# Pairwise heads in the hybrid layers of a two-block transformer kernel on one Trainium2 core

## The chip, the cores and the metric

The kernel runs on one core of one Trainium2 chip. Its time is the device time of one execution in microseconds; a comparison uses the median of several runs. Engines are named as in the profile: PE (TensorE), DVE (VectorE), ACT (ScalarE), POOL (GpSimd), SP (the queue that issues the DMAs).

## What is computed

Batch 1, 512 tokens, width 1024, everything in float32. The first block (two layers with feed-forward parts, one stick-breaking attention, one recurrent mixer) isn't touched. The second block is two hybrid layers and a norm. One hybrid layer, cut to what matters:

```
h = rmsnorm_2(x, norm_g)
proj = h @ w_in                      # a_q a_k a_v a_g  b_q b_k b_v b_g  i_q i_k i_w  c_q c_k c_v c_g  m_g
ya = moba_attention(rope(a_q), rope(a_k), a_v)            # 6 heads of 64, causal at this length
yb = dsa_attention(rope(b_q), rope(b_k), b_v, rope(i_q), rope(i_k), i_w)   # 6 heads, one key head; top 128 keys by an index score
yc = dilated_mixture(rope(c_q), rope(c_k), c_v)           # 3 groups x 4 heads, dilation 1, 4, 16; groups mixed by their log sums
merged = sigmoid(m_g)[0] * ((ya * silu(a_g)) @ w_br_a) + ... b ... + ... c ...
x = x + merged @ w_out
```

Each head is a softmax attention: scores, row maximum, exponentials with row sums, division by the sum, product with the values.

## The kernel before, in words

Every engine has its own hand-written program (`tensor`, `scalar`, `vector`, `gpsimd`, `sync`), and these meet by named semaphore steps. The order of the work is thus the order in which each program's loops are written; an engine that waits holds back all that is behind it.

Weight products are split: a panel of 256 weight columns (1 MB) is loaded by SP, rounded by ACT (`w_high`, L1239), the remainder taken by DVE (`w_low`, L1772), and PE makes three matmuls for each of the eight k-tiles and each half of the panel (48 matmuls 128x512, L594, in `product`). There are three `w_high` buffers and four raw ones.

In `hybrid(layer)` (stages `h0` and `h1`) the heads come after six panels. There are 24 heads in `L.heads`: six A, six B, then four C for each of three groups. A step `i` of the loop runs, on PE: `turns(i - 2)` (transposes of the finished weights, L1064), the panel of `L.fills` if there is one (16 of them stand beside the heads: queries, keys, values and gates of the heads to come), `scores(i + 1)` (L1048 for A and B, L1041 and L1044 for C), `values(i - 2)` (L1086, L1082). A and B heads are causal triangles of 1280 columns (TRI); C heads have 896 or 512.

On DVE a step runs `row_max(i)` (scores from PSUM with scale and mask, L2287; maxima, L2292 and L2295), `weights(i - 1)` (L2300, L2303), the rope arithmetic of the last panel (L2195 to L2199), `w_low` of the next one, up to six `some` rounds (L2237, L2239: the top keys for B, 48 rounds in all, 27 of them beside heads), and the gate of a finished pair of heads (L2342, L1958). On ACT: `turned_copy(i - 2)` (L1591: transposed weights back into the one buffer `L.PT`), `exps(i - 1)` (L1597), eviction of the panel (L1534 for rope, L1540 for gates), `w_high` of the next one. DVE copies 256 of the 1280 transposed columns (L2313). The scores of a head lie in PSUM columns 0 to 1279, its transposed weights in 1280 to 2559; bank 5 takes the products with the values, banks 6 and 7 the panels. Head dimension is 64, so a score matmul uses one half of the array's rows and a value matmul one half of its columns, in the code by `r0`:

```
m = e.matmul(flat[:, ROW_AT[n]:ROW_AT[n] + P * (n + 1)], L.q_of(kind, ti)[r0:r0 + HD, n * P:(n + 1) * P], ...)
m = e.matmul(psum[r0:r0 + HD, OUT, kt * P:S], L.v_of(kind, h, kt), L.PT[:, COL_AT[kt]:COL_AT[kt] + S - P * kt], ...)
```

The first block's attention (`stick_breaking`, stage `sb`) already takes its heads two by two; its value matmuls (L870) alternate between the two heads of a pair.

After the heads every engine meets at a fence, and PE turns the log sums (L1145).

## Time and profile before

| | |
|---|---|
| median of 3 runs | 3378.89 us (3375.52 to 3392.6) |
| the profiled execution | 3381.35 us, its span 3379.6 us |
| PE busy | 3220.0 us, 95% of the span |
| DVE busy | 1769.8 us, 52% |
| ACT busy | 1168.1 us, 35% |
| mean granted TensorE clock | 0.969 |

A busy matmul engine isn't one at its peak: matmuls overlap in the records, so that their start-to-start distance is their price. The chain that ended last is 84% PE, 9% DVE and 4% ACT.

### The profile page before, as it was taken

To read this page: it belongs to the slowest core of one execution; us is meant where nothing else is said; L and a number is where in the kernel's file an instruction comes from. 1 tells how busy PE (TensorE), PEld (TensorE's weight loads), DVE (VectorE), ACT (ScalarE), POOL (GpSimd) and SP (SyncE) were. 2 spreads that over 40 slices of the span, in tenths; PEclk is the share of its full clock that TensorE was granted. 3 is DMA by queue.
4 is the path that set the end of the run, shared out by engine and by line. 5 is a ranking of instruction groups with operands and counts; after the bars stand their busy time and mean duration, and the time that the engine had idled before them with its cause. 6 is when DMAs were issued, how large, how long until landed. Compare 5 with 4: busy or idle time off the path is not lost.

```text
span 3379.6 us, 38726 instructions
## 1 busy us (share of the span) xinstructions
PE 3220.0 (95%) x16353; PEld 2662.9 (79%) x16353; DVE 1769.8 (52%) x2488; ACT 1168.1 (35%) x1532; POOL 167.5 (5%) x228
## 2 busy tenths in 40 slices
PE   6999999999999999999999998889989998899899
PEld 5888888798888888887888887656768886567688
DVE  6545543355555543367632346875553458755534
ACT  4222356532223223247421233333442332335322
POOL 0000012200000000012000000000000010000000
PEclk8999999999999999999999998989989999899899
DMA  6555421135554432232222322221212232222132
GB/s 220 185 189 191 133 88 51 38 113 176 194 178 150 162 125 93 88 110 71 92 91 96 100 75 82 80 74 53 67 58 92 81 95 76 69 63 70 56 100 69
DMA packets 287270, 354.23 MB, mean 105 GB/s; under 512 B 9546, under 2 KB 263290, under 8 KB 287098
## 3 DMA queue, kind: packets, MB, share of 16 engines
q1 hardware_dynamic: 287098, 351.75, 32.1%
q8 instruction: 130, 2.13, 0.3%
q14 instruction: 42, 0.34, 0.0%
HBM read 336.52 MB, written 2.10 MB: 100 GB/s over the span
## 4 chain that ended last, share of the span: by engine, by line
PE 84%; DVE 9%; ACT 4%; issue 1%; DMA 1%; POOL 1%; SPq 0%; DVEq 0%; ACTq 0%; POOLq 0%
PE psum L594 56%; PE psum L753 6%; PE psum L711 3%; PE psum L1181 3%; PE psum L635 2%; PE psum L615 2%; PE psum L1048 2%; PE psum L1086 2%; PE psum L851 1%; DVE w_low L1772 1%; PE psum L1064 1%; DVE area L2239 1%; DVE psum L1921 1%; PE psum L560 1%; DVE h_low L1931 1%
## 5 line engine op out<-in xcount | busy, mean ns | idle before, releaser
L594 PE MATMUL psum<-h_high,w_high 128*128 128x512 f32 x2400 | 947.8, 395 | 27.9 <-DVE y_plain L2206 11.6
L594 PE MATMUL psum<-h_low,w_high 128*128 128x512 f32 x2400 | 941.0, 392 | 0.0
L594 PE MATMUL psum<-h_high,w_low 128*128 128x512 f32 x2400 | 940.2, 392 | 0.0
L1772 DVE TENSOR_TENSOR w_low<-raw,w_high 128x2048 fp32r<-128x2048 f32 (+2 forms) x246 | 547.6, 2235 | 301.0 <-ACT w_high L1239 300.8
L1239 ACT CAST w_high<-raw 128x2048 fp32r<-128x2048 f32 (+3 forms) x254 | 464.5, 1841 | 521.5 <-DMA raw<-in_ffn_w_gu 234.6
L594 PEld LDWEIGHTS psum<-h_high,w_high 128*128 128x128 f32 x2400 | 454.1, 189 | 131.9 <-DVE y_plain L2206 12.1
L594 PEld LDWEIGHTS psum<-h_high,w_low 128*128 128x128 f32 x2400 | 453.9, 189 | 97.3
L594 PEld LDWEIGHTS psum<-h_low,w_high 128*128 128x128 f32 x2400 | 454.1, 189 | 94.9 <-issue 1.0
L594 PE MATMUL psum<-y_high,w_high 128*128 128x512 f32 x592 | 232.9, 393 | 7.5 <-DVE y_low L1958 3.6
L2044 DVE TENSOR_TENSOR area<-area,psum 128x512 f32<-128x512 f32 x88 | 60.2, 684 | 340.1 <-PE psum L594 331.7
L594 PE MATMUL psum<-y_high,w_low 128*128 128x512 f32 x592 | 231.4, 391 | 0.0
L594 PE MATMUL psum<-y_low,w_high 128*128 128x512 f32 x592 | 231.3, 391 | 0.0
L1308 ACT CAST y_high<-area 128x512 fp32r<-128x512 f32 x102 | 62.7, 620 | 442.3 <-DVE area L2044 403.1
L1963 DVE SCALAR_TENSOR_TENSOR xT<-psum,gain_out,xT 128x512 f32<-128x512 f32 (+1 forms) x156 | 90.7, 623 | 199.4 <-PE psum L594 159.3
L1789 DVE SCALAR_TENSOR_TENSOR mod_acc<-raw,vec,mod_acc 128x1024 f32<-128x1024 f32 x112 | 143.9, 1285 | 60.8 <-DMA raw<-in_mod_w 55.6
L711 PE MATMUL psum<-h_high,w_high 128*128 128x256 f32 x448 | 133.1, 297 | 10.4 <-DVE h_low L1931 4.6
L753 PE MATMUL psum<-y_high,w_high 128*128 128x256 f32 x480 | 138.2, 288 | 0.1
L594 PEld LDWEIGHTS psum<-y_high,w_high 128*128 128x128 f32 x592 | 111.7, 189 | 32.2 <-ACT y_high L1308 4.0
L753 PE MATMUL psum<-y_high,w_low 128*128 128x256 f32 x480 | 136.4, 284 | 0.0
L753 PE MATMUL psum<-y_low,w_high 128*128 128x256 f32 x480 | 136.4, 284 | 0.0
L594 PEld LDWEIGHTS psum<-y_high,w_low 128*128 128x128 f32 x592 | 111.7, 189 | 23.7
L594 PEld LDWEIGHTS psum<-y_low,w_high 128*128 128x128 f32 x592 | 111.7, 189 | 23.1 <-issue 0.2
(301 smaller groups left out, 4584.4 us busy)
## 6 DMA issues: line engine op xcount, KB each, us to landing
raw<-in_ffn_w_gu SPq DMA_DIRECT2D x88, 1024.0 KB, 5.6
raw<-in_mod_w SPq DMA_DIRECT2D x64, 1024.0 KB, 5.0
raw<-in_w_in SPq DMA_DIRECT2D x64, 1024.0 KB, 5.2
raw<-in_ffn_w_down SPq DMA_DIRECT2D x32, 1024.0 KB, 7.4
raw<-in_ffn_w_down SPq DMA_DIRECT2D x16, 768.0 KB, 4.7
raw<-in_sb_w_qkv SPq DMA_DIRECT2D x12, 1024.0 KB, 5.1
area<-area SPq DMA_DIRECT2D x92, 128.0 KB, 2.3
raw<-in_lru_w_in SPq DMA_DIRECT2D x10, 1024.0 KB, 5.3
```

The lines of the kernel that those rows point to most:

```text
L594: mm = e.matmul(psum[0:width, base + m, :], wv[a][:, at_k, c0:c0 + width], X[b][:, k, :], start=(at_k == 0 and (a, b) == (0, 0)), stop=(at ...
L615: mm = e.matmul(psum[:, base + m, :], wv[a][:, at_k, m * P:(m + 1) * P], X[b][:, k, :], start=(at_k == 0 and (a, b) == COMBOS[0]), stop=(a ...
L635: mm = e.matmul(flat[:, o:o + n], X[b][:, k, tt * P:(tt + 1) * P], wv[a][:, k, :], start=(k == 0 and (a, b) == (0, 0)), stop=(k == KD - 1 ...
L711: mm = e.matmul(psum[:, base + m, HALF[h]], wv[a][:, k, m * P:(m + 1) * P], H[b][:, k, HALF[h]], start=first, stop=last)
L753: mm = e.matmul(psum[:, bank, m * S // 2:(m + 1) * S // 2], wv[a][:, at_k, m * P:(m + 1) * P], X[b][:, k, HALF[h]], start=(at_k == 0 and ( ...
L1048: m = e.matmul(flat[:, ROW_AT[n]:ROW_AT[n] + P * (n + 1)], L.q_of(kind, ti)[r0:r0 + HD, n * P:(n + 1) * P], L.k_of(kind, h)[:, 0:P * (n + ...
L1086: m = e.matmul(psum[r0:r0 + HD, OUT, kt * P:S], L.v_of(kind, h, kt), L.PT[:, COL_AT[kt]:COL_AT[kt] + S - P * kt], start=kt == 0, stop=kt = ...
L1181: mm = e.matmul(psum[:, base + m, :], wv[x][:, k, m * P:(m + 1) * P], Y[y][:, k, :], start=(k == k0 and (x, y) == (0, 0)), stop=(k == k1 - ...
L1239: e.copy(w_high[x % NW][:, :n], raw[raw_at[m]][:, :n]).then_inc(*q.up(s_high, "w_high", x))
L1772: e.tensor_tensor(w_low[raw_at[m]][:, :n], raw[raw_at[m]][:, :n], w_high[x % NW][:, :n].bitcast(F32), ALU.subtract).then_inc(*q.up(s_low, ...
L1789: g = e.scalar_tensor_tensor(mod_acc[:, :], w, c, mod_acc[:, :], ALU.mult, ALU.add)
L1963: return e.scalar_tensor_tensor(dst, src, gain_out[:, j:j + 1], dst, ALU.mult, ALU.add)
```

## The change

`L.heads` becomes `L.pairs`, twelve pairs of heads in another order of kinds: A A A, C C (dilation 1), B B B, C C (4), C C (16). A step handles two heads: both their scores, all their transposes, both products with the values. Matmuls of head 0 (array rows or columns 0 to 63) and head 1 (64 to 127) alternate. The scores of a pair take five banks, and the transposed weights go back into those same banks for A, B and C of dilation 1 (`turned_at`), so that `turn_weights(p)` waits until DVE has taken the scores of pair `p + 1`, and `scores(p + 2)` until ACT has copied the transposed weights of `p`. ACT copies all columns, back into the softmax buffers (four now, `L.PT` is gone). A panel's two halves (`panel_tiles`) stand at two places of a step, by the table `L.beside`; `w_high` and `w_low` are made two panels ahead, not one. The panels are loaded in another order. `dilated_mask`, ropes and gates move with them. Before and after the heads nothing changes.

```diff
-        IN_HEADS = ((("b_q", 0), 256), (("b_q", 256), 256), (("b_g", 0), 256), (("b_g", 256), 128), (("c_q", 0), 256), (("c_k", 0), 256),
-                    (("c_v", 0), 256), (("c_q", 256), 256), (("c_k", 256), 256), (("c_v", 256), 256), (("c_q", 512), 256),
+        IN_HEADS = ((("c_q", 0), 256), (("c_k", 0), 256), (("b_g", 256), 128), (("b_q", 0), 256), (("b_q", 256), 256), (("c_v", 0), 256),
+                    (("b_g", 0), 256), (("c_q", 256), 256), (("c_k", 256), 256), (("c_v", 256), 256), (("c_q", 512), 256),
                     (("c_k", 512), 256), (("c_v", 512), 256), (("m_g", 0), 256), (("m_g", D), 256), (("c_g", 0), 256), (("m_g", 2 * D), 256))
...
-            L.SS, L.PT, L.score = [tiles(ss + TRI * i, TRI) for i in range(3)], tiles(pt, TRI), tiles(sc, TRI)
+            L.SS, L.score = [tiles(ss + TRI * i, TRI) for i in range(4)], tiles(sc, TRI)
...
-            L.heads = [(kind, h, 0) for kind in "AB" for h in range(6)] + [("C", h, g) for g in range(3) for h in range(4)]
-            L.fills = {0: ("rope", "b_q", 0), 1: ("rope", "b_q", 256), 2: ("gate", "b_g", 0), 4: ("gate", "b_g", 256), 5: ("rope", "c_q", 0),
-                       6: ("rope", "c_k", 0), 8: ("tokens", "c_v", 0), 9: ("rope", "c_q", 256), 12: ("rope", "c_k", 256),
-                       13: ("turned", "c_v", 256), 15: ("rope", "c_q", 512), 16: ("rope", "c_k", 512), 18: ("turned", "c_v", 512),
-                       20: ("merge", "m_g", 0), 21: ("merge", "m_g", D), 23: ("gate", "c_g", 0)}
...
+            L.pairs = ([("A", ti, 0) for ti in range(3)] + [("C", ti, 0) for ti in range(2)] + [("B", ti, 0) for ti in range(3)]
+                       + [("C", ti, g) for g in (1, 2) for ti in range(2)])
+            L.beside = {
+                -1: ([("c_q", 0, (0, 1))], []),
+                0: ([("c_k", 0, (0, 1))], [("b_g", 256, (0,))]),
+                1: ([("b_q", 0, (0, 1))], [("b_q", 256, (0,))]),
+                2: ([("b_q", 256, (1,))], [("b_q", 256, "turn"), ("c_v", 0, (0,))]),
+                3: ([("c_v", 0, (1,))], [("b_g", 0, (0,))]),
+                4: ([("b_g", 0, (1,))], [("c_q", 256, (0,))]),
+                5: ([("c_q", 256, (1,))], [("c_k", 256, (0,))]),
+                6: ([("c_k", 256, (1,))], [("c_v", 256, (0, 1))]),
+                7: ([("c_v", 256, "turn")], [("c_q", 512, (0, 1))]),
+                8: ([("c_k", 512, (0, 1))], [("c_v", 512, (0,))]),
+                9: ([("c_v", 512, (1,))], [("c_v", 512, "turn")]),
+                10: ([("m_g", 0, (0, 1))], [("m_g", D, (0,))]),
+                11: ([("m_g", D, (1,))], [("c_g", 0, (0, 1))]),
+                12: ([], []),
+            }
...
+            def score_at(p, x):
+                kind, ti, g = L.pairs[p]
+                return x * (TRI if kind != "C" else 1024 if g == 0 else 512)
+            def turned_at(p, x):
+                kind, ti, g = L.pairs[p]
+                return score_at(p, x) + (1024 if kind == "C" and g else 0)
...
+                def scores(p):
+                    kind, ti, g = L.pairs[p]
+                    if p:
+                        for x in range(2):
+                            q.wait_ge(*at("scores_taken", stage, p - 1, x))
+                    if p > 1:
+                        for x in range(2):
+                            q.wait_ge(*at("turned_taken", stage, p - 2, x))
...
+                        for x, n in ((0, 1), (1, 3), (0, 3), (1, 2), (0, 2), (1, 0), (0, 0), (1, 1)):
+                            if (x, n) == (1, 1):
+                                q.wait_ge(*at("scores_begun", stage, p))
+                            r0, o = x * HD, L.score_at(p, x) + ROW_OF[x][n]
+                            m = e.matmul(flat[:, o:o + P * (n + 1)], L.q_of(kind, ti)[r0:r0 + HD, n * P:(n + 1) * P],
+                                         L.k_of(kind, 2 * ti + x)[:, 0:P * (n + 1)], start=True, stop=True)
+                            if (x, n) == (0, 1):
+                                m.then_inc(*q.up(s_attend, "scores_begun", stage, p))
+                    m.then_inc(*q.up(s_attend, "scores", stage, p))
...
+                def turn_weights(p):
+                    for x in range(2):
+                        q.wait_ge(*at("weights", stage, p, x))
+                    if p:
+                        for x in range(2):
+                            q.wait_ge(*at("turned_taken", stage, p - 1, x))
+                    if p + 1 < n_pairs and L.turned_at(p, 0) == 0:
+                        for x in range(2):
+                            q.wait_ge(*at("scores_taken", stage, p + 1, x))
+                    shared = L.pairs[p][0] != "C"
+                    for x in range(2):
+                        blocks = L.turns(p, x)
+                        for i, (src, dst) in enumerate(blocks):
+                            o = L.turned_at(p, x) + dst
+                            m = e.transpose(flat[:, o:o + P], L.SS[2 * (p % 2) + x][:, src:src + P], ident[:, :])
+                            if (x, i) == ((1, 1) if shared else (0, len(blocks) - 1)):
+                                m.then_inc(*q.up(s_turn, "weights_turned", stage, p, 0))
+                    m.then_inc(*q.up(s_turn, "weights_turned", stage, p, 1))
...
+                            for x in range(2):
+                                c = COL_OF[x][kt]
+                                m = e.matmul(psum[x * HD:(x + 1) * HD, OUT, kt * P:S], L.v_of(kind, 2 * ti + x, kt), w[x][:, c:c + S - P * kt],
+                                             start=kt == 0, stop=kt == NT - 1, skip_group_check=True)
+                    m.then_inc(*q.up(s_attend, "head_out", stage, p))
...
-                scores(0)
-                for i in range(n_heads + 2):
-                    if i >= 2:
-                        turns(i - 2)
-                    fill_rest(i - 1)
-                    fill(i)
-                    if i + 1 < n_heads:
-                        scores(i + 1)
-                    if i >= 2:
-                        values(i - 2)
...
+                for p in range(-1, n_pairs):
+                    if p + 1 < n_pairs:
+                        scores(p + 1)
+                    beside(p, 0)
+                    if p >= 0:
+                        turn_weights(p)
+                    beside(p, 1)
+                    if p >= 0:
+                        values(p)
...
+                def cast(p, w):
+                    for name, c0 in L.begun(p, w):
+                        split_to(two_ahead_of(number[stage, name, c0]))
+                def turned_copy(p, x):
+                    top = L.width(p)
+                    q.wait_ge(*at("weights_turned", stage, p, x))
+                    o = L.turned_at(p, x)
+                    e.copy(L.SS[2 * (p % 2) + x][:, 0:top], flat[:, o:o + top]).then_inc(*q.up(s_act, "turned_taken", stage, p, x))
...
-                n_heads = len(L.heads)
-                for i in range(n_heads + 2):
-                    if i >= 2:
-                        turned_copy(i - 2)
-                    if 1 <= i <= n_heads:
-                        exps(i - 1)
-                    fill_rest(i - 1)
-                    fill(i)
-                    if i >= 2:
-                        finish(i - 2)
...
+                for p in range(-1, n_pairs + 1):
+                    beside(p - 1, 1)
+                    cast(p, 0)
+                    if p >= 1:
+                        finish(p - 1)
+                    if p + 1 < n_pairs:
+                        for x in range(2):
+                            exps(p + 1, x)
+                        for x in range(2):
+                            log_sum(p + 1, x)
+                    beside(p, 0)
+                    if 0 <= p < n_pairs:
+                        for x in range(2):
+                            turned_copy(p, x)
+                    cast(p, 1)
...
+                rounds_of, n_pairs = {-1: 3, 0: 7, 1: 4, 2: 6}, len(L.pairs)
...
+                def take_scores(p, x):
+                    kind, ti, g = L.pairs[p]
+                    buf, width, o = L.SS[2 * (p % 2) + x], L.width(p), L.score_at(p, x)
...
+                    if p > 1:
+                        q.wait_ge(*at("head_out", stage, p - 2))
+                    runs = [(0, ROW_AT[1], o + 2 * P), (ROW_AT[1], TRI, o)] if kind != "C" and x else [(0, width, o)]
+                    for a, b, at_ in runs:
+                        m = e.scalar_tensor_tensor(buf[:, a:b], flat[:, at_:at_ + b - a], SCALE, mask[:, a:b], ALU.mult, ALU.add)
+                    m.then_inc(*q.up(s_vec, "scores_taken", stage, p, x))
...
-                n_heads = len(L.heads)
-                for i in range(n_heads + 2):
-                    if i >= 2:
-                        turned_copy(i - 2)
-                    if i < n_heads:
-                        row_max(i)
-                    if 1 <= i <= n_heads:
-                        weights(i - 1)
-                    fill_rest(i - 1)
-                    fill(i)
-                    if i in beside:
-                        beside[i]()
-                    if i >= 2:
-                        finish(i - 2)
...
+                for p in range(-1, n_pairs + 1):
+                    if p + 1 < n_pairs:
+                        for x in range(2):
+                            take_scores(p + 1, x)
+                    if p >= 1:
+                        gate_out(p - 1)
+                    if p + 1 < n_pairs:
+                        for x in range(2):
+                            row_max(p + 1, x)
+                    beside(L.early(p))
+                    lows(p, 0)
+                    if p + 1 < n_pairs:
+                        for x in range(2):
+                            weights(p + 1, x)
+                    beside(L.rest(p))
+                    if p >= 1:
+                        finish(p - 1)
+                    if p + 1 < n_pairs:
+                        for x in range(2):
+                            lse_add(p + 1, x)
+                    lows(p, 1)
+                    some(rounds_of.get(p, 0))
+                    if p == 3:
+                        select()
```

What moves on PE, in the first hybrid layer. Before, at the second and third A head (scores L1048, values L1086 of one head, transposes L1064 of the next):

```order
L1048 MATMUL psum<-area 128x128
L1048 MATMUL psum<-area 128x256
L1048 MATMUL psum<-area 128x384
L1048 MATMUL psum<-area 128x512
L1086 MATMUL psum<-area 64x512
L1086 MATMUL psum<-area 64x384
L1086 MATMUL psum<-area 64x256
L1086 MATMUL psum<-area 64x128
L1064 MATMUL psum<-ident,area 128x128 x10
```

Now, at the first A pair's values (L1173) and the third pair's scores (L1119), between two panels:

```order
L1173 MATMUL psum<-area 64x512 x2
L1173 MATMUL psum<-area 64x384 x2
L1173 MATMUL psum<-area 64x256 x2
L1173 MATMUL psum<-area 64x128 x2
L1119 MATMUL psum<-area 128x256
L1119 MATMUL psum<-area 128x512 x2
L1119 MATMUL psum<-area 128x384 x2
L1119 MATMUL psum<-area 128x128 x2
L1119 MATMUL psum<-area 128x256
```

Each value matmul now stands next to its twin of the other head, and the eight score matmuls of two heads are interleaved with sizes that differ.

On ACT, before, at two B heads (rope eviction L1534, transposed copy L1591, exponentials L1597):

```order
L1534 COPY area<-psum 128x1024
L1591 COPY area<-psum 128x1024
L1597 ACTIVATE area,mod_acc<-area,mod_acc 128x128
L1597 ACTIVATE area,mod_acc<-area,mod_acc 128x256
L1597 ACTIVATE area,mod_acc<-area,mod_acc 128x384
L1597 ACTIVATE area,mod_acc<-area,mod_acc 128x512
L1308 CAST y_high<-y_plain 128x512
```

Now, at the step of a B pair (L1719 exponentials, L1651 rope eviction, L1712 transposed copies, L1356 `w_high`):

```order
L1719 ACTIVATE area,mod_acc<-area,mod_acc 128x128
L1719 ACTIVATE area,mod_acc<-area,mod_acc 128x256
L1719 ACTIVATE area,mod_acc<-area,mod_acc 128x384
L1719 ACTIVATE area,mod_acc<-area,mod_acc 128x512
L1651 COPY area<-psum 128x1024
L1712 COPY area<-psum 128x1280 x2
L1356 CAST w_high<-raw 128x2048
```

The transposed copies of a pair stood ahead of the next exponentials and now stand behind both heads' exponentials and the eviction.

On DVE, now, the same step (L2418 scores taken, L2428 and L2431 maxima, L2436 and L2439 weights, L1901 `w_low`):

```order
L2418 SCALAR_TENSOR_TENSOR area<-psum,area 128x1280
L2418 SCALAR_TENSOR_TENSOR area<-psum,area 128x1024
L2418 SCALAR_TENSOR_TENSOR area<-psum,area 128x256
L2428 TENSOR_REDUCE mod_acc<-area 128x1 x4
L2431 TENSOR_SCALAR mod_acc<-mod_acc 128x4
L2428 TENSOR_REDUCE mod_acc<-area 128x1 x4
L2431 TENSOR_SCALAR mod_acc<-mod_acc 128x4
L2436 RECIPROCAL mod_acc<-mod_acc 128x4
```

The 12 copies of 256 columns per layer (L2313) are gone from DVE, and each second A or B head's scores are taken in two instructions.

## Rows read from the trace of the kernel before

**Rows 1.** The page: span, and busy time of the engines.

```profile
span 3379.6 us, 38726 instructions
...
PE 3220.0 (95%) x16353; PEld 2662.9 (79%) x16353; DVE 1769.8 (52%) x2488; ACT 1168.1 (35%) x1532; POOL 167.5 (5%) x228
```

**Rows 2.** Timeline of PE, where the heads begin and end, both layers.

```profile
2155.67 0.55 PE L1048 MATMUL psum<-area 64*128 64x128 f32 x1 [4.76 <-DVE y_plain L2206]
...
2491.13 2.72 PE L1145 MATMUL psum<-ident,mod_acc 128*4 128x128 f32 x12 [1.10 <-ACT area L1659]
...
2822.65 0.76 PE L1048 MATMUL psum<-area 64*128 64x128 f32 x2 [5.94 <-DVE y_plain L2206]
...
3152.70 0.58 PE L1145 MATMUL psum<-ident,mod_acc 128*4 128x128 f32 x2 [1.10 <-ACT area L1659]
```

**Rows 3.** Busy times in the first layer's heads (us, PE, PEld, DVE, ACT, POOL, PEclk, DMA).

```profile
2151.00:2490.00 339.00, 303.24 (x1424) 227.18 (x1424) 209.45 (x422) 137.33 (x290) 17.65 (x23) 0.93 0.22 64
```

**Rows 4.** Timeline of PE: the end of a panel and one B head.

```profile
2273.01 0.39 PE L594 MATMUL psum<-h_low,w_high 128*128 128x512 f32 x1
2273.24 0.39 PE L594 MATMUL psum<-h_high,w_low 128*128 128x512 f32 x1
2273.56 2.42 PE L1048 MATMUL psum<-y_plain 64*128 64x128 f32 x8
2275.91 2.37 PE L1086 MATMUL psum<-area 128*64 128x512 f32 x8
2278.21 1.31 PE L1064 MATMUL psum<-ident,area 128*128 128x128 f32 x10
```

**Rows 5.** Timeline of PE: the scores of one C head of dilation 1.

```profile
2371.68 1.83 PE L1041 MATMUL psum<-area 64*128 64x128 f32 x14
```

**Rows 6.** Timeline of PE: values of a pair in the first block.

```profile
524.26 0.64 PE L870 MATMUL psum<-area 128*64 128x512 f32 x1
524.27 0.64 PE L870 MATMUL psum<-causal,area 128*64 128x512 f32 x1
...
526.57 0.50 PE L851 MATMUL psum<-sb_parts,neg_parts 128*128 128x512 f32 x1
```

**Rows 7.** Timeline of DVE: first two A heads, the work beside them.

```profile
2160.42 1.49 DVE L2287 SCALAR_TENSOR_TENSOR area<-psum,causal 128x1280 f32<-128x1280 f32 x1 [5.01 <-PE psum L1048]
...
2163.72 2.29 DVE L1772 TENSOR_TENSOR w_low<-raw,w_high 128x2048 fp32r<-128x2048 f32 x1
2165.92 0.42 DVE L2237 MAX8 small<-area 128x8 f32<-128x256 f32 x1
...
2169.29 0.42 DVE L2237 MAX8 small<-area 128x8 f32<-128x256 f32 x1
...
2180.39 0.17 DVE L2300 RECIPROCAL mod_acc<-mod_acc 128x4 f32<-128x4 f32 x1
...
2181.79 0.68 DVE L2196 TENSOR_TENSOR area<-area,rope_s 128x512 f32<-128x512 f32 x1
...
2185.05 2.28 DVE L1772 TENSOR_TENSOR w_low<-raw,w_high 128x2048 fp32r<-128x2048 f32 x1
```

**Rows 8.** Timeline of DVE: a dilated rope, from its first instruction to the next `w_low`.

```profile
2403.62 0.68 DVE L2196 TENSOR_TENSOR area<-area,rope_s 128x512 f32<-128x512 f32 x1
...
2408.12 2.28 DVE L1772 TENSOR_TENSOR w_low<-raw,w_high 128x2048 fp32r<-128x2048 f32 x1
```

**Rows 9.** Timeline of ACT: gate eviction, transposed copy, exponentials of an A head.

```profile
2230.63 1.28 ACT L1540 ACT_TABLE_LOAD   x1
...
2238.51 1.01 ACT L1591 COPY area<-psum 128x1024 f32<-128x1024 f32 x1 [4.68 <-PE psum L1064]
2239.41 0.40 ACT L1597 ACTIVATE area<-area,mod_acc 128x128 f32<-128x128 f32 x1
...
2241.61 1.89 ACT L1239 CAST w_high<-raw 128x2048 fp32r<-128x2048 f32 x1
```

**Rows 10.** Timeline of PE: an A head's scores after a wait.

```profile
2228.24 4.63 PE L1048 MATMUL psum<-area 64*128 64x128 f32 x8 [3.44 <-DVE area L2287]
```

More of the change, by code:

```diff
@@ new lines, in hybrid_views, with last_tile, begun, done @@
+            kinds = {"b_g": "gate", "c_g": "gate", "m_g": "merge", "c_v": "turned"}
+            L.what = lambda name, c0: "tokens" if (name, c0) == ("c_v", 0) else kinds.get(name, "rope")
+            def last_tile(name, c0):
+                return 0 if (name, c0) == ("b_g", 256) else 1
+            def begun(p, w):
+                return [(name, c0) for name, c0, ms in L.beside[p][w] if ms != "turn" and 0 in ms]
+            def done(p, w):
+                if p < -1:
+                    return []
+                return [(name, c0) for name, c0, ms in L.beside[p][w] if ms != "turn" and last_tile(name, c0) in ms]
@@ new lines, in turned, with early, rest @@
+            def turned(p, w):
+                if p < -1:
+                    return []
+                return [(name, c0) for name, c0, ms in L.beside[p][w] if ms == "turn"]
+            put_off = [("c_q", 0), ("c_k", 0)]
+            def early(p):
+                out = [u for u in (done(p - 1, 0) if p > -1 else []) if u in put_off]
+                return out + (done(p - 1, 1) if p > -1 else [])
+            def rest(p):
+                return [u for u in done(p, 0) if u not in put_off]
+            L.begun, L.done, L.turned, L.early, L.rest, L.last_tile = begun, done, turned, early, rest, last_tile
@@ new lines, in beside, with gate_out @@
+                def beside(units):
+                    for name, c0 in units:
+                        what = L.what(name, c0)
+                        if what == "rope":
+                            place = L.place_of.get((name, c0))
+                            rope_rest(name, c0, *([] if place is None else [("scores_taken", stage, place, x) for x in range(2)]))
+                        if what == "gate":
+                            gate_rest(name, c0)
+                def gate_out(p):
+                    kind, ti, g = L.pairs[p]
+                    if kind == "C":
+                        return
```

444 lines of the change are left out of this document (221 added, 223 removed).

## The prediction

> **What bounds the kernel now.** I read the page first. PE is busy for 95% of the span [rows 1] and holds 84% of the chain that ended last, so a gain must shorten PE's program or its waits. The change touches only the heads of the two hybrid layers. On PE's timeline these run from 2155.67 to 2491.13 us and from 2822.65 to 3152.70: 335.5 and 330.1 us [rows 2], a fifth of the span. Both ends are matmuls of lines that stay, so I count from the one to the other.
>
> Then I priced PE's work in there, by distances from start to start. A panel's matmul takes 0.23 us, a full panel of 48 of them 11.1 [rows 4]. One A or B head takes 2.35 for scores, 2.30 for values and 1.07 for ten transposes (1.31 less the tail of the last) [rows 4]. A C head of dilation 1 takes 1.76 for its 14 score records, 0.126 each [rows 5]; I take that price for the other C matmuls: about 1.75 for values, 1.0 and 1.0 in a dilated head, with 0.107 per transpose. With 15.5 panels that is 172 + 12 x 5.7 + 4 x 4.3 + 8 x 2.45 + 2.5 for turned value columns = 280 us. The stretch takes 335, so 55 us are waits and low clock. DVE is busy for 209 of 339 us and ACT for 137, and the granted clock is 0.93 on average [rows 3]. Nothing else is full, but DVE's 209 are bunched: the key-selection rounds lie beside the first heads.
>
> **The change, part by part.** *Matmuls side by side.* A pair's two heads use different halves of the array. The first block shows what that is worth: two value matmuls start at 524.26 and 524.27, and a pair's whole set is done at 526.57, 2.3 us after it began [rows 6], which is what one head takes in the hybrid layer [rows 4]. So values halve. Scores have mixed sizes in an order where each head's pieces sum to 1280 columns; I take them as halved too. Bounds: 2.35 per A or B pair if they overlap fully, 4.7 if not. The saving per layer is 6 x (2.35 + 2.30) + 2 x 3.5 + 4 x 2.0 = 43 us; if scores do not overlap at all it is 21. PE's floor falls to 280 - 43 = 237 us per layer.
>
> *Can DVE follow?* Prices from its timeline: taking an A head's scores and its maxima 3.3 (of it 1.5 for the taking), `w_low` 2.2, three rounds 3.37, so 1.12 each, weights 1.4, a rope panel 3.3 [rows 7], or 4.5 when dilated [rows 8]. The gating of a pair costs about 1.2, from the same widths. A pair with C of dilation 1 costs 4.6 and 2.5 in place of 6.6 and 2.8, by its 896 of 1280 columns. By the new tables, DVE's steps cost
> -1: 6.6 + 2.8 + 1.5 `w_low` 3.3 + 3 rounds 3.4 = 16;
> 0: 6.6 + 2.8 + rope 3.3 + 4.4 + 7 rounds 7.8 = 25;
> 1: 6.6 + 2.8 + two ropes and a gate 7.1 + 4.4 + 4 rounds 4.5 + 1.2 = 27;
> 2: 4.6 + 2.5 + 3.3 + 2.2 + 6 rounds 6.7 + 1.5, and 1.4 of waiting for exponentials = 22;
> 3: 4.6 + 2.5 + 2.2 + 7 rounds and the mask 9.1 + 1.5 + 1.4 = 21.
> That is 111 us, where PE has 95 us of work in the same steps. So DVE becomes the bound there. `w_low` also stands behind a cast that ACT makes after its transposed copies; in steps 0 and 3 DVE gets there first, 5 us together. Removing the 256-column copies saves DVE some 5 us per layer, half of it in this stretch (already left out above).
>
> *The new waits.* `turn_weights(p)` waits for the taking of pair p + 1 and `scores(p + 2)` for the copies of p, which stand behind both exponentials on ACT. So a step can't be shorter than: taking 3.0, first maxima 1.8, two heads' exponentials at 2.2 [rows 9], an eviction 1.0, two copies of 1280 columns at 1.15 (0.9 per 1024 [rows 9]), values 2.3, scores 2.35, hops 0.6: 17.8 us. Steps 0 to 3 are longer anyway. Steps 4 and 5 have only 14 to 17.5 us of DVE work, so the loop bounds them: 18.6 (the gate eviction with table loads, 1.28 each [rows 9], makes it longer, C's narrower copies shorter) and 17.8. A panel's half stands between transposes and values, and hides nothing beyond 5.5 us.
>
> *The rest.* From there on DVE has 10 to 20 us per step beside 18 to 23 of PE, and PE is the bound: 105 us of matmuls, with about 5 of waits, chiefly for the rope of `c_k` 512, whose queries and keys are due one step after their panel (eviction 1.0, swap DMA, rope 4.5, against 7.5 us of PE work). At the end the last gate is evicted on ACT between two table loads before the last output copy, and the fence waits for it: 5 us, where now it waits 1.1 [rows 2]. POOL's and SP's moved steps (ropes' cosine, swaps, loads) have far more room: POOL is busy for 18 of 339 us [rows 3].
>
> *The clock.* After a wait of 3.4 us an A head's scores took 4.63 us, twice the 2.42 of a full clock [rows 10, 4]: the lower level, 1.2 GHz. New waits of 3 to 6 us stand in steps 2 to 5. Where DVE is the bound this costs nothing, in the loop of steps 4 and 5 it does; I add 6 us (bounds 0 and 25, the latter if turning, values and scores run at half clock in every loop and some panels behind them).
>
> **The sum.** Per layer 5 (first scores, slow as now [rows 10]) + 111 + 5 + 36.4 + 110 + 5 + 6 = 278 us. That is 57 less than 335.5 and 52 less than 330.1, together 109. From the profiled execution's 3381.35 us this gives 3272; its own time lies 2.5 above the median of the runs, so I forecast **3270 us**, 3.2% faster. About 0.5% is what a measurement of this kernel can tell from no change.
>
> **The rivals.**
> *PE bound throughout.* If DVE's backlog were absorbed by the depth of the pipeline, the layer would take 237 + 10 = 247 us, and the kernel 3381 - 171 = 3210. Against it: the banks are shared, so PE can be at most one pair ahead. Chance 0.07.
>
> *Copies bound it.* The transposed copies are ACT's alone now, and every A, B and early C step closes a loop through them. If hops, evictions and low clock make that loop 24 us rather than 17.8, steps 2 to 7 gain nothing from DVE's spare time: 20 us more per layer, 3310. For it: these waits did not exist; ACT idles long before L1591 today [rows 9]. Against it: only two steps have less DVE work than 17.8. The Trainium skill, TensorEngine Tiling (Array Packing), section PSUM Bottleneck, says that tiling speeds up TensorE but not the evacuation of PSUM, which may then become the bound, and advises sharing it between ScalarE and VectorE; the change does the opposite, and by this rule the time would be this rival's. Chance 0.2.
>
> *The pairs do not overlap.* If alternating matmuls ran one after another, the 43 us would stay on PE; DVE's bound hides some 20 of them. 278 + 23 to 278 + 43 gives 3315 to 3355. The first block speaks against it for values [rows 6]; for scores nothing shown is as clear. Chance 0.08.
>
> *Slower: the clock stays low.* More waits per matmul could keep PE at 1.2 GHz. The stage breaks even when 55 us are lost; as about 25 us of slack take up the first losses, some 80 of its 237 us of matmuls have to run at half clock that now run at full. If all 140 us up to step 6 did, the layer would take 278 + 115 and the kernel 3500. Against it: today's section waits as much (55 of 335 us) and is still granted 0.93 [rows 3]. The Trainium skill's page TensorE: Matmul & The Clock Gate, section HAM oscillation, warns of just this, bursts of matmuls between waits, each begun at the lower clock; the trace has single cases of it [rows 10], no lasting one. Chance 0.05.
>
> **How the numbers follow.** Forecast 0.6, PE bound 0.07, copies 0.2, no overlap 0.08, slow clock 0.05. The range takes the forecast's bounds (loop and clock at +25 per layer: 3320; scores cheap and DVE quick at -22 per layer: 3226), which holds the copies' case too: 3225 to 3325. Left out are most of the first, third and fourth rival. Faster by over 0.5% is everything but the slow clock and a strip around no change: 0.93; same 0.02, slower 0.05.
>
> **What would show it.** In the new profile: each layer's heads shortened to about 278 us; pair values at 2.3 us and pair scores near 2.4; DVE without gaps until some 120 us into the heads, PE waiting there for it at the transposes; then PE dense from the third B pair on; a wait near 5 us before the log sums. Pair scores near 4.7, or a granted clock under 0.85 in the heads, would speak for the rivals. Equal lengths of the two layers' gains show that nothing outside matters; a change before 2155 us or behind the fence would prove me wrong about the scope.

## The result, and the profile after

The changed kernel takes **3336.9 us** (3335.7 to 3342.5), the kernel before 3381.9 beside it: ratio 0.987, 95% interval 0.984 to 0.990. It is faster, by 45 us (1.3%) and not by the 109 forecast, and lies above the range.

Of the page of the changed kernel these rows answer to [rows 1]; the group of panel matmuls and the chain are added:

```profile
span 3334.6 us, 38716 instructions
...
PE 3123.2 (94%) x16353; PEld 2617.1 (78%) x16353; DVE 1752.0 (53%) x2476; ACT 1173.2 (35%) x1532; POOL 180.1 (5%) x228
...
PE 77%; DVE 13%; ACT 5%; DMA 1%; issue 1%; POOL 1%; SPq 1%; DVEq 0%; ACTq 0%; POOLq 0%
...
L1204 PE MATMUL psum<-h_high,w_high 128*128 128x512 f32 x464 | 194.1, 418 | 78.8 <-DVE y_plain L2335 45.0
```

PE is busy for 97 us less than before (3220.0), but the span falls by 45.0 only: half of the saved work came back as waits. The last row says where PE waits, for 78.8 us in all: before matmuls of L1204, the heads' panels, and most of it for DVE's gating at L2335. My sum has no such term.

PE's timeline from the first scores to the transposes of the log sums, as in [rows 2]. For the first layer these are all waits over 2 us ahead of its instructions, but for one of 3.13 us at 2273.03 for DVE's taking of scores; of the second layer only the first and the last row are shown:

```profile
2155.24 1.22 PE L1119 MATMUL psum<-area 64*128 64x256 f32 x3 [5.05 <-DVE y_plain L2335]
...
2211.62 0.76 PE L1204 MATMUL psum<-h_high,w_high 128*128 128x512 f32 x1 [14.09 <-DVE y_plain L2335]
...
2250.91 0.69 PE L1221 MATMUL psum<-ident,area 64*128 64x64 f32 x4 [4.39 <-ACT area L1651]
...
2279.88 0.77 PE L1204 MATMUL psum<-h_high,w_high 128*128 128x512 f32 x1 [4.52 <-ACT area L1740]
...
2307.61 0.77 PE L1204 MATMUL psum<-h_high,w_high 128*128 128x512 f32 x1 [8.14 <-DVE y_plain L2335]
...
2329.53 0.47 PE L1204 MATMUL psum<-h_high,w_high 128*128 128x512 f32 x1 [2.46 <-ACT area L1651]
...
2353.83 0.76 PE L1204 MATMUL psum<-h_high,w_high 128*128 128x512 f32 x1 [5.39 <-ACT area L1651]
...
2378.19 0.47 PE L1204 MATMUL psum<-h_high,w_high 128*128 128x512 f32 x1 [3.37 <-ACT area L1764]
...
2414.91 1.44 PE L1111 MATMUL psum<-area,y_plain 64*128 64x128 f32 x10 [3.06 <-DVE area L2328]
...
2469.54 1.47 PE L1262 MATMUL psum<-ident,mod_acc 128*4 128x128 f32 x12 [2.41 <-ACT area L1783]
...
2798.58 1.23 PE L1119 MATMUL psum<-area 64*128 64x256 f32 x3 [5.92 <-DVE y_plain L2335]
...
3109.22 1.04 PE L1262 MATMUL psum<-ident,mod_acc 128*4 128x128 f32 x8 [2.42 <-ACT area L1783]
```

The heads take 314.3 and 310.6 us: 21.2 and 19.4 less than in [rows 2], where 278 was forecast. That is 40.6 of the 45.0 us; of the rest 2.5 lie between the two layers' heads and 1.5 behind them. Inside the first layer's heads PE is busy for 258.6 us instead of 303.3 and idle for 55.7 instead of 32.2. Seven waits between 2211 and 2379, 42.4 us together, stand before a panel's first matmul (or, at L1221, before the small transposes that use the same banks). All panels and these transposes go through one pair of PSUM banks, 6 and 7, and `wait_free(6)` holds PE until the panel before has been taken out of them. Both banks come free together, by the one eviction or gating that stands behind the panel's second half.

DVE's timeline shows why the longest of them lasts 14 us. The panel of `b_g` 256 was full long before; its gating is the instruction of L2335:

```profile
2200.54 2.94 DVE L2418 SCALAR_TENSOR_TENSOR area<-psum,causal 128x1280 f32<-128x1280 f32 x3
2203.40 0.68 DVE L2471 TENSOR_TENSOR y_plain<-y_plain,psum 128x512 f32<-128x512 f32 x1
2203.99 1.66 DVE L2428 TENSOR_REDUCE mod_acc<-area 128x1 f32<-128x128 f32 x4
...
2207.53 0.69 DVE L2325 TENSOR_TENSOR area<-area,rope_s 128x512 f32<-128x512 f32 x1
...
2210.79 0.68 DVE L2335 TENSOR_TENSOR y_plain<-y_plain,psum 128x512 f32<-128x512 f32 x1
...
2230.13 0.69 DVE L2325 TENSOR_TENSOR area<-area,rope_s 128x512 f32<-128x512 f32 x1 [13.67 <-DMA area<-area]
...
2241.92 2.08 DVE L2418 SCALAR_TENSOR_TENSOR area<-psum,mod_acc 128x896 f32<-128x896 f32 x2
```

The 0.68 us of gating stand in `early(1)`, behind seven rounds of step 0, then the taking of the third pair's scores, a pair's gating, maxima and a rope. PE starts `b_q` 0 only at 2211.62. Then DVE itself waits 13.67 us, for the swap of that late panel (the DMA that a rope needs ahead of its arithmetic), and the engine that I thought full in step 1 is idle for a third of it.

On ACT's timeline the wait of 5.39 us looks so (L1719 are exponentials, L1651 the eviction of `c_q` 256; PE ran that panel's second half from 2339.83 to 2345.57):

```profile
2331.53 1.92 ACT L1356 CAST w_high<-raw 128x2048 fp32r<-128x2048 f32 x1
2346.55 0.62 ACT L1425 CAST y_high<-y_plain 128x512 fp32r<-128x512 f32 x1 [13.10 <-DVE y_plain L2471]
2348.33 0.40 ACT L1719 ACTIVATE area<-area,mod_acc 128x128 f32<-128x128 f32 x1 [1.16 <-DVE mod_acc L2431]
...
2352.70 0.99 ACT L1651 COPY area<-psum 128x1024 f32<-128x1024 f32 x1
```

ACT is idle for 13 us, nearly all of it while the panel is still being computed, so it is not overloaded. Yet the eviction comes 7 us after the panel is complete, since it stands in program order behind a cast and both heads' exponentials, which wait 1.16 us for DVE first.

The matmuls themselves are as forecast (PE's timeline: scores, values, scores of C with dilation 1, transposes, each of a whole pair):

```profile
2171.63 2.43 PE L1119 MATMUL psum<-area 64*128 64x256 f32 x16
...
2232.39 2.37 PE L1173 MATMUL psum<-area 128*64 128x512 f32 x16
2234.70 1.83 PE L1111 MATMUL psum<-area 64*128 64x128 f32 x28
...
2244.14 2.38 PE L1140 MATMUL psum<-ident,area 128*128 128x128 f32 x20 [1.93 <-DVE area L2418]
```

A pair's scores take 2.43 us, where one head took 2.42; values 2.37 for 2.37; C's 28 records 1.83, where 14 took 1.83 [rows 4, 5]. (The trace has two records for each of these matmuls on half of the array, and one for each transpose.) The window over the heads, in the columns of [rows 3]:

```profile
2151.00:2470.00 319.00, 259.09 (x1429) 206.83 (x1430) 202.34 (x415) 142.31 (x291) 17.75 (x17) 0.91 0.24 69
```

### The profile page after: what moved, and what is told of

The parts are those of the page before. It is cut to its first block, busy times and chain, and to the rows that moved or that the text cites. A ratio compares the mean times of both kernels' runs of the same rounds, so it can differ in the third digit from the quotient of the medians.

```text
span 3334.6 us, 38716 instructions
## 1 busy us (share of the span) xinstructions
PE 3123.2 (94%) x16353; PEld 2617.1 (78%) x16353; DVE 1752.0 (53%) x2476; ACT 1173.2 (35%) x1532; POOL 180.1 (5%) x228
## 4 chain that ended last, share of the span: by engine, by line
PE 77%; DVE 13%; ACT 5%; DMA 1%; issue 1%; POOL 1%; SPq 1%; DVEq 0%; ACTq 0%; POOLq 0%
PE psum L654 48%; PE psum L1204 7%; PE psum L813 6%; PE psum L771 3%; PE psum L1298 3%; PE psum L675 2%; DVE w_low L1901 2%; DVE area L2368 2%; ACT area L1719 1%; PE psum L695 1%; PE psum L911 1%; DVE small L2366 1%; DVE area L2418 1%; DVE psum L2050 1%; DVE mod_acc L2428 1%
## 5 line engine op out<-in xcount | busy, mean ns | idle before, releaser
L654 PE MATMUL psum<-h_high,w_high 128*128 128x512 f32 (+1 forms) x1936 | 759.5, 392 | 9.5 <-DVE w_low L1901 4.0
L654 PE MATMUL psum<-h_high,w_low 128*128 128x512 f32 (+1 forms) x1936 | 755.9, 390 | 0.0
L654 PE MATMUL psum<-h_low,w_high 128*128 128x512 f32 (+1 forms) x1936 | 755.7, 390 | 0.0
L1901 DVE TENSOR_TENSOR w_low<-raw,w_high 128x2048 fp32r<-128x2048 f32 (+2 forms) x246 | 547.8, 2236 | 357.1 <-ACT w_high L1356 357.0
L1356 ACT CAST w_high<-raw 128x2048 fp32r<-128x2048 f32 (+4 forms) x254 | 464.7, 1843 | 525.2 <-DMA raw<-in_ffn_w_gu 237.4
L654 PEld LDWEIGHTS psum<-h_high,w_high 128*128 128x128 f32 (+1 forms) x1936 | 364.2, 188 | 90.2 <-issue 6.2
L654 PEld LDWEIGHTS psum<-h_high,w_low 128*128 128x128 f32 (+1 forms) x1936 | 363.9, 188 | 77.4
L654 PEld LDWEIGHTS psum<-h_low,w_high 128*128 128x128 f32 (+1 forms) x1936 | 364.4, 188 | 76.8 <-issue 1.0
L1204 PE MATMUL psum<-h_high,w_high 128*128 128x512 f32 x464 | 194.1, 418 | 78.8 <-DVE y_plain L2335 45.0
L1204 PE MATMUL psum<-h_low,w_high 128*128 128x512 f32 x464 | 188.8, 407 | 0.0
L1204 PE MATMUL psum<-h_high,w_low 128*128 128x512 f32 x464 | 188.2, 406 | 0.0
L1204 PEld LDWEIGHTS psum<-h_high,w_high 128*128 128x128 f32 x464 | 92.5, 199 | 104.4 <-issue 83.9
```

The lines of the kernel that those rows point to most:

```text
L654: mm = e.matmul(psum[0:width, base + m, :], wv[a][:, at_k, c0:c0 + width], X[b][:, k, :], start=(at_k == 0 and (a, b) == (0, 0)), stop=(at ...
L1204: mm = e.matmul(psum[:, 6 + m, :], wv[a][:, k, m * P:(m + 1) * P], H[b][:, k, :], start=(k == 0 and (a, b) == COMBOS[0]), stop=(k == KD - ...
L1356: e.copy(w_high[x % NW][:, :n], raw[raw_at[m]][:, :n]).then_inc(*q.up(s_high, "w_high", x))
L1901: e.tensor_tensor(w_low[raw_at[m]][:, :n], raw[raw_at[m]][:, :n], w_high[x % NW][:, :n].bitcast(F32), ALU.subtract).then_inc(*q.up(s_low, ...
```

## The experiments

Two theories stood after the result. **Banks**: the time is lost where banks 6 and 7 wait for an eviction or a gating that stands behind the next pair's softmax on an in-order engine; moving that instruction gives it back. **DVE load**: DVE's work in steps -1 to 3 sets the pace and the bank waits are where it shows; moving work about on DVE brings nothing. A third, from the forecast's rivals, was that ACT's copies bound the later steps. The kernel before took 3378.9 to 3381.9 us beside them.

| run | on top of | us | ratio, 95% interval | first layer's heads, us |
|---|---|---|---|---|
| changed kernel | | 3336.9 | 0.987 (0.984 to 0.990) | 314.3 |
| e1_gate_early | changed | 3319.9 | 0.981 (0.979 to 0.983) | 304.0 |
| e2_evict_first | changed | 3312.9 | 0.979 (0.977 to 0.981) | 297.8 |
| e5_both | e1 and e2 | 3292.8 | 0.973 (0.971 to 0.975) | 288.0 |
| e7_both_gate0 | e5 | 3275.5 | 0.969 (0.967 to 0.971) | 280.6 |
| e10_best | e7 | 3262.7 | 0.965 (0.963 to 0.967) | 273.9 |
| e3_serial | changed | 3371.3 | 0.997 (0.995 to 0.999) | 329.0 |
| e11_serial | e7 | 3309.0 | 0.978 (0.976 to 0.981) | 298.0 |
| e4_no_rounds | changed | 3305.0 | 0.977 (0.975 to 0.979) | 295.1 |
| e6_both_no_rounds | e5 | 3248.8 | 0.961 (0.959 to 0.964) | 266.4 |
| e8_dve_copies | changed | 3338.3 | 0.987 (0.985 to 0.990) | 315.0 |
| e9_one_ahead | e7 | 3279.9 | 0.970 (0.968 to 0.972) | 283.1 |

### e1: the gate of `b_g` 256 one place earlier

```diff
-                    beside(L.early(p))
+                    beside([u for u in L.early(p) if u != ("b_g", 256)])
...
                     some(rounds_of.get(p, 0))
+                    if p == 0:
+                        beside([("b_g", 256)])
```

> The changed kernel, except that DVE does the gate of panel b_g 256 at the end of step 0 instead of behind the next pair's scores, maxima and rope. Theory 'banks' (PE's next panel can't start until ACT and DVE have emptied banks 6 and 7, and they come to it late): the 14.1 us wait before panel b_q 0 shrinks to about 4, 8 to 10 us less per layer, 3319 (3315 to 3323). Theory 'DVE load' (the sum of DVE's work in steps -1 to 3 sets the pace, as forecast): DVE's sum is the same, so 3335 to 3338.

17.0 us faster, though DVE has the same work. PE's timeline where the wait of 14.09 was:

```profile
2201.42 0.47 PE L1204 MATMUL psum<-h_high,w_high 128*128 128x512 f32 x1 [3.84 <-DVE y_plain L2335]
```

One instruction of 0.68 us, moved 10 us forward, is worth 8.5 us per layer. This is what the banks theory asked for; DVE load had 3335 to 3338.

### e2: ACT evicts ahead of the exponentials

In ACT's loop `beside(p, 0)` stands ahead of `exps(p + 1, x)` for `p` in 2 to 6, and not behind them.

> The changed kernel, except that in steps 2 to 6 ACT evicts the first panel of a step ahead of the next pair's exponentials, not behind them. Theory 'banks': the waits of 4.4, 4.5, 8.1, 2.5 and 5.4 us before half panels shrink by some 3 each, 10 to 15 us less per layer, 3307 to 3317. Theory 'DVE load', or the loop through the transposed copies: nothing, or up to 4 us more, since the exponentials come 1 us later: 3336 to 3341.

24.0 us faster: again the banks. PE's timeline of this run shows what is late next:

```profile
2268.79 3.22 PE L1140 MATMUL psum<-ident,area 128*128 128x128 f32 x14 [5.53 <-DVE area L2421]
...
2292.78 3.22 PE L1140 MATMUL psum<-ident,area 128*128 128x128 f32 x14 [4.48 <-DVE area L2421]
```

The waits of 4.39 and 4.52 for evictions are gone. In their place the transposes wait longer for DVE's taking of the next pair's scores, the wait that the forecast had named (1.93 and 3.13 us were the longest in the changed kernel). The gating that cost 8.14 us is not moved by this edit; its wait is still 5.71.

### e5 and e7: both, and then the gate of `b_g` 0

> Both edits together. Theory 'banks': the gains add up nearly, 3288 to 3302. Theory 'DVE load': 3333 to 3341.

44.1 us faster than the changed kernel, where 17.0 and 24.0 add to 41. Its trace still had this wait in step 4, the same pattern a third time:

```profile
2289.69 0.76 PE L1204 MATMUL psum<-h_high,w_high 128*128 128x512 f32 x1 [5.78 <-DVE y_plain L2338]
```

So e7 makes this gating ahead of the next pair's weights on DVE:

```diff
                     lows(p, 0)
+                    if p == 4:
+                        beside(L.rest(p))
                     if p + 1 < n_pairs:
                         for x in range(2):
                             weights(p + 1, x)
-                    beside(L.rest(p))
+                    if p != 4:
+                        beside(L.rest(p))
```

> Both reorderings, and also the gating of b_g 0 on DVE in step 4 ahead of the next pair's weights instead of behind them. Banks theory: the PE wait of 5.8 us for it shrinks to 1 to 3 us, and 2 to 5 us per layer come back: 3283 to 3289. If that wait only passes to the next (loop-bound step, transposes waiting for DVE's taking): 3291 to 3294.

17.3 us more, against the 2 to 5 per layer expected. The heads became only 7.4 us shorter in the first layer (288.0 to 280.6) and 7.0 in the second (288.6 to 281.6). That is 14.4 us in the profiled executions, whose spans differ by 12.5; e7's enters its first heads 4.8 us later than e5's, at 2159.4, ahead of anything that the edit moves. The remaining 3 us or so of the medians are not explained, and lie within their intervals. It is still more than the wait alone offered, which fell from 5.78 to 1.59, 4.2 us per layer:

```profile
2286.09 3.08 PE L1140 MATMUL psum<-ident,area 128*128 128x128 f32 x14 [5.68 <-DVE area L2421]
2290.77 0.47 PE L1204 MATMUL psum<-h_high,w_high 128*128 128x512 f32 x1 [1.59 <-DVE mod_acc L2439]
```

The first matmul behind the shorter wait takes 0.47 us, not 0.76, the next ones 0.39, not 0.63, and the panel's half 5.72 us, not 7.68: PE no longer falls to the lower clock there. With three kinds of placement changed and not an instruction removed, the layer takes 280.6 us, and the kernel 3275.5, where 278 and 3270 were forecast.

### e4 and e6: no selection rounds

The 27 rounds beside the heads are left out of the computation (`rounds.clear()` after those ahead of the heads), once in the changed kernel and once in e5.

> The changed kernel without the 27 selection rounds that DVE makes beside the heads of each layer (left out of the computation, some 30 us of DVE work per layer at 1.12 us each). DVE-load theory (the forecast's term: steps -1 to 3 last as long as DVE's work in them, 111 us, and not PE's 95): 16 us per layer or more come back, 3295 to 3307. Banks theory (panel banks 6 and 7 wait for a gate or an eviction that stands behind the next pair's softmax on an in-order engine): the waits move but stay in part, since the gate still stands behind taking, maxima and rope of the next pair; 5 to 13 us per layer come back, 3311 to 3327.

> The same rounds left out of the kernel with both reorderings (gate of b_g 256 early, evictions ahead of the exponentials), which measured 3292.8. Its trace shows PE waits of 3.9, 1.9, 5.1 and 5.6 us that end on DVE in steps 1 to 3. DVE-load theory: with the bank waits gone, the load of steps -1 to 3 is what bounds there, and 16 to 20 us per layer come back: 3253 to 3261. If banks or the loop still bound these steps: less than 8 us per layer, 3277 to 3290.

31.9 us on the changed kernel and 44.0 on e5. The first falls in what DVE load expected, and is more than the banks theory gave it (3311 at best). It does not contradict e1: the gating that PE waits for stood behind seven of these rounds, so that removing them also frees the bank earlier (the wait of 14.09 is 11.13 in e4). Both theories hold a part, and I had set them too far apart. What e6 adds is that DVE's load is worth more, 22 us per layer, once the banks don't hide it; that is more than the 16 to 20 expected. The gain lies in the steps where the rounds stood: steps -1 to 3 take 118.2 us in e5 and 96.3 in e6, where the forecast had 111 for DVE's work and 95 for PE's. In its trace PE's waits for the taking of scores have all but gone (from the view of waits of the heads, two rows of e6, then one of e5):

```profile
PE psum L1204 <- DVE y_plain L2338: 8.1, 1, 8.1
...
PE psum L1140 <- DVE area L2422: 0.8, 2, 0.5
```

```profile
PE psum L1140 <- DVE area L2421: 13.5, 5, 5.6
```

The first row is the gating of `b_g` 0 again, which e7 moves and e6 does not.

### e8: copies on DVE

From step 4 on, DVE makes both transposed copies of a pair, behind the next pair's weights, and ACT none:

```diff
-                        for x in range(2):
+                        for x in range(2 if p < 4 else 0):
                             turned_copy(p, x)
...
                             weights(p + 1, x)
+                    if 4 <= p < n_pairs:
+                        for x in range(2):
+                            turned_copy(p, x)
```

> The changed kernel, but from step 4 on DVE makes both transposed copies of a pair, not ACT. Copies theory (the rival of the forecast: ACT's exponentials, evictions and copies in a row bound steps 4 to 7, some 20 us per layer): at least 8 us per layer come back, 3321 or less. Banks theory: the values never wait for a copy for long; only the evictions behind the copies come 2.3 us earlier on ACT, two to four times: 0 to 4 us per layer, 3329 to 3337, or slower by as much where DVE's own queue is lengthened.

No change (3338.3 against 3336.9): the copies theory falls. Nor does PE wait for a copy in the changed kernel: of all its matmul waits in the heads none names L1712. The edit has a cost of its own in step 4, where the wait for the gating grows from 8.14 to 9.20 us, but 1 us is far from the 8 per layer that this theory asked for. The wait of step 5 is the same to the hundredth, since the eviction stands ahead of the copies and behind the exponentials:

```profile
2355.06 0.77 PE L1204 MATMUL psum<-h_high,w_high 128*128 128x512 f32 x1 [5.39 <-ACT area L1651]
```

### e9: weights one panel ahead

`two_ahead_of` becomes `ahead_of` in the heads' `cast` and `lows`, on top of e7.

> The kernel with all three reorderings (3275.5), with w_high and w_low of the heads' panels made one panel ahead, as before the change, not two. If casting two ahead is what keeps PE and DVE from waiting for ACT's cast behind the exponentials: 3 us per layer or more are lost, 3281 to 3305. If one panel ahead is early enough, since a panel takes 11 us and a cast 1.9: 3272 to 3279.

3279.9 against e7's 3275.5, with intervals that overlap, and between the two expectations (from 3281, up to 3279): at most a small gain lies in the second panel ahead. The run does not tell 0 from 4 us.

### e3 and e11: one head after the other

The matmuls of a pair are put in the order head 0, then head 1, in scores and values. The transposes, which e11's expectation names too, stayed as they are. For scores of A and B:

```diff
-                        for x, n in ((0, 1), (1, 3), (0, 3), (1, 2), (0, 2), (1, 0), (0, 0), (1, 1)):
+                        for x, n in ((0, 1), (0, 3), (0, 2), (0, 0), (1, 3), (1, 2), (1, 0), (1, 1)):
```

> The changed kernel with the two heads' score and value matmuls one head after the other instead of alternating; nothing else moves. If alternation is what halves them, PE has 43 us more of matmuls per layer; some of it falls where PE waits anyway, so 25 to 43 us more per layer, 3387 to 3423. Theory 'no overlap' (alternation is worth nothing, the gain came from fewer waits): 3335 to 3340.

> All three reorderings, and a pair's matmuls one head after the other in scores, transposes and values, as in the run before this that took 3371 us. That run's trace priced a lone head at 3.8 to 3.9 us where a pair side by side takes 2.4, some 27 us of PE work per layer, and 17 of them reached the time. If the bank waits hid the rest, without them nearly all reaches it: 20 to 27 us per layer, 3315 to 3330. If DVE's load hides it as before: 12 to 18 us per layer, 3299 to 3312.

A pair's scores in e3, from PE's timeline, then a pair's values and the scores of a pair of C with dilation 1:

```profile
2201.07 3.82 PE L1119 MATMUL psum<-area 64*128 64x256 f32 x16
...
2236.40 3.93 PE L1174 MATMUL psum<-area 128*64 128x512 f32 x16
2240.26 3.05 PE L1111 MATMUL psum<-area 64*128 64x128 f32 x28
```

3.82 us for 2.43, 3.93 for 2.37 and 3.05 for 1.83. The time, 3371.3, is below the 3387 to 3423 expected. PE's busy time rises from 3123.2 to 3184.9 on the page, 31 us per layer, and the time by 34.4, 17 per layer. In e11 it rises by 26 per layer (3116.5 to 3168.2) and the time by 33.5, again 17. I had thought that the bank waits hid the rest, so that without them nearly all would reach the time. They hid a small part at most: 17 of 31 us reach it with them, 17 of 26 without. In e11's view of waits the transposes wait 5.2 us for DVE's taking, where e7, with the matmuls side by side, has 13.8:

```profile
PE psum L1140 <- DVE area L2422: 5.2, 3, 2.6
```

```profile
PE psum L1140 <- DVE area L2421: 13.8, 4, 5.7
```

Of the 9 us per layer that do not reach the time in e11, 8.6 are found here: the slower matmuls fill time in which PE would wait for DVE. With pairs one head after the other the whole change would be worth 0.3%.

### e10: the best version

On top of e7 ACT evicts first in step 7 too, and DVE gates `b_g` 256 between the fourth and the fifth round of step 0.

> All three reorderings, the eviction ahead of the exponentials in step 7 too, and the gate of b_g 256 on DVE between the fourth and the fifth round of step 0, not behind all seven. The trace shows PE waits of 4.4 us for that gate and 3.4 us for the turned copy of step 7. Banks theory: 3 to 6 us per layer come back, 3263 to 3270. If DVE's load (the next transposes' wait for its taking) absorbs the first of them: 3268 to 3273. If neither counts: 3274 to 3277.

3262.7 us: 12.8 below e7 and just past the lower end of what was expected (3263), 74 below the changed kernel and 116 below the kernel before. The wait of 14.09 is 0.52 now, and of the page's 78.8 us before L1204 7.9 are left:

```profile
L1204 PE MATMUL psum<-h_high,w_high 128*128 128x512 f32 x464 | 189.2, 408 | 7.9 <-DVE mod_acc L2439 2.9
```

```profile
2198.08 0.47 PE L1204 MATMUL psum<-h_high,w_high 128*128 128x512 f32 x1 [0.52 <-DVE y_plain L2338]
...
2230.47 2.37 PE L1140 MATMUL psum<-ident,area 128*128 128x128 f32 x20 [2.94 <-DVE area L2421]
...
2254.48 3.22 PE L1140 MATMUL psum<-ident,area 128*128 128x128 f32 x14 [5.30 <-DVE area L2421]
...
2278.48 3.22 PE L1140 MATMUL psum<-ident,area 128*128 128x128 f32 x14 [4.39 <-DVE area L2421]
```

What is left in the early steps are waits for DVE's taking of scores, where DVE's load decides.

## Why the prediction was wrong

DVE's steps, from the taking of one pair's scores to the next, with PE's first scores ahead and the stretch to the log sums behind:

| | first | -1 | 0 | 1 | 2 | 3 | 4 | 5 | rest | sum |
|---|---|---|---|---|---|---|---|---|---|---|
| forecast | 5 | 16 | 25 | 27 | 22 | 21 | 18.6 | 17.8 | 121 | 278 with 5 for casts |
| changed kernel | 4.8 | 15.9 | 24.6 | 41.4 | 28.9 | 23.8 | 24.6 | 23.7 | 126.6 | 314.3 |
| e7 | 4.2 | 15.9 | 25.0 | 31.1 | 24.2 | 23.1 | 17.6 | 20.8 | 118.7 | 280.6 |

*Right: the matmuls.* The pairs overlap fully, scores too, and PE's busy time in the heads fell by 44.6 and 45.9 us in the two layers (303.3 to 258.6, 301.9 to 256.0), where I removed 43; the other 6 of the page's 97 us lie outside the heads. That term needed the overlap of scores, for which [rows 6] speak only by way of the values; it came out at the end of its bounds that was taken.

*Right: DVE's prices.* Steps -1 and 0 last 15.9 and 24.6 us for 16 and 25, and step 1, freed of its bank wait, 27.0 in e10 for 27. DVE's load bounds the early steps, as e6 shows by leaving out rounds: steps 1 to 3 get 18 us shorter (77.0 in e5 to 58.8). In step 0 this bound is close to the next one: without its seven rounds, 7.8 us by my price, it still takes 23.5.

*Wrong: the panels' banks.* The step that failed is the sentence "A panel's half stands between transposes and values, and hides nothing beyond 5.5 us", together with the rest of its part on new waits. I worked out the loops through the five score banks and took each panel as ready to run wherever it stood in PE's order. But banks 6 and 7 make a loop of their own: a panel's last matmul, its eviction or gating, the next panel. The change puts up to one panel beside each half step, and left the eviction at a place in ACT's or DVE's program where both heads' softmax is ahead of it. This loop bounds step 1 (41.4 for 27) and steps 4 and 5 (24.6 and 23.7 for 18.6 and 17.8), and adds in steps 2 and 3. Steps 1 to 5 together take 36 us more than their entries in the forecast; the first layer as a whole missed by 36, since what the forecast had too much for casts and too little behind step 5 nearly cancels. Reordering alone took 33.7 us off, to 280.6 in e7: 25.6 of them in steps 1 to 5 and 7.9 in step 6 (28.0 to 20.1). What e7 still has above the forecast in steps 1 to 3, 8.4 us, is not all banks: there the transposes wait for DVE's taking of scores.

*Wrong: the loop of steps 4 and 5 as the bound.* It was not what ended last in the changed kernel, where banks 6 and 7 were. With these out of the way, e7 takes 17.6 and 20.8 us for 18.6 and 17.8, and e10 19.6 and 20.8. The loop is thus of about the size that I gave it, but no run shows that it is what bounds these steps.

*The clock.* I added 6 us. The granted clock of the window is 0.91 with 314 us of heads, and 0.95 in e10, and PE's busy time for the same matmuls is 259.1 us and 251.7: about 7 us are the price of the lower clock that goes with the longer waits, beside the waits themselves. The slow-clock rival's comparison was off: its 55 us of waits before the change are waits and low clock together, and PE's idle time alone was 32.2 us.

*The tail.* 5 us were forecast for the wait before the log sums; it is 2.4, and 1.9 in e3 and e11.

*The rivals.* The nearest in time, "copies bound it" at 3310, named a step of 24 us, and steps 4 and 5 take 24.6 and 23.7. It was right in kind, that ACT's program holds up PE, and wrong in place: e8 took the copies away from ACT and nothing moved, so the agreement of the numbers is chance. The Trainium skill, TensorEngine Tiling (Array Packing), section PSUM Bottleneck, says that emptying PSUM may become the bound once tiling has made TensorE faster. That held here in the sense that PE waits for banks to be emptied. But ACT is busy for 142.3 of 319 us in the window, and sharing the work with VectorE, the section's advice, gave nothing for the copies in e8; moving the evictions ahead, with the same engine and the same work, gave 24 us in e2. "The pairs do not overlap" is excluded by the rows and by e3: with a pair's matmuls one head after the other the kernel is 34 us slower. "PE bound throughout" had 247 us per layer; even e10 takes 273.9. The slow clock didn't come.

The range failed as well. I had taken its bounds from the prices of known terms, and left no room for a wait of another resource: the three placements of e7 alone cost 61 us (3336.9 to 3275.5), more than the 55 between the forecast and the upper end of 3325.

## What to carry to other kernels

When a change makes PE's work shorter, list every group of PSUM banks that is reused within a step, and for each write down PE's last write, the instruction that empties it, and everything ahead of that instruction in its engine's program; do this for the banks beside the change too, not only for those that it touches. An eviction of 1 us belongs ahead of the long work of the next step, also on an engine that is idle more than half of the time. And a load on an engine and a wait that it feeds can't be told apart by taking the load away: move the waited-for instruction alone, with the load unchanged.

## What the runs showed of the hardware that was not expected

- Matmuls of two heads on the two halves of the array overlap fully even where their sizes come in another order (256, 512, 384, 128 columns for one head, 512, 384, 128, 256 for the other): 2.43 us for 16 records, where one head's 8 took 2.42.
- In e3's order, one head after the other, the pair takes 3.82 us for scores and 3.93 for values, not twice 2.42 and 2.37. So some of the two heads' work still overlaps, or a head alone has a cost that isn't paid twice; no run separates these.
- Lengthening PE's work by 31 and 26 us per layer (e3, e11) cost 17 both times. Removing some 30 us of DVE work per layer brought 16 and 22 (e4, e6). In this section no engine's work is worth its own length.
